# A hybrid decoder step on one core: the samples' state recurrence moved into the input projection, the group norm placed right behind the scan, and branch B taken last in each output tile

## The reference

```
s_kk = S @ kk
S = S * w[None, :] - s_kk[:, None] * (kk * a)[None, :] + v[:, None] * k[None, :]
o = S @ r
```

## Time and profile before

| | |
|---|---|
| median of 3 runs | 1962.02 us (1960.63 to 1970.27) |
| profiled execution | 1961.91 us, span 1960.1 us |
| TensorE busy | 1801.5 us (92%) |
| weight loads | 1092.4 us (56%) |
| VectorE busy | 817.9 us (42%) |
| ScalarE busy | 478.5 us (24%) |
| mean granted TensorE clock | 0.967 |
| DMA | 298.62 MB, mean 152 GB/s |

### The profile page before, as it was taken

How to read it: one execution, slowest core, us unless ns; L and a number is a source line. 1 busy time by engine, 2 the same in 40 slices (tenths; PEclk the granted TensorE clock), 3 DMA queues, 4 the chain that set the end, 5 groups by cost and what they waited for, 6 DMA issues and landing times.

```text
span 1960.1 us, 34623 instructions
## 1 busy us (share of the span) xinstructions
PE 1801.5 (92%) x14642; PEld 1092.4 (56%) x14642; DVE 817.9 (42%) x1662; ACT 478.5 (24%) x855; POOL 170.1 (9%) x220
## 2 busy tenths in 40 slices
PE   6999999999999999979999997887788786999997
PEld 3555555555554556746776775666667342444442
DVE  4450799732213350036556533444434864111112
ACT  4301100010526231125554531111112231100000
POOL 1000000011000005600000000000000001111110
PEclk9999999999999999989999998998989798999999
DMA  6222321385230535141100057777776536878782
GB/s 224 78 105 80 118 87 64 121 196 158 92 120 33 204 153 206 50 152 39 54 1 1 2 175 224 221 236 218 213 226 193 226 100 230 296 272 277 277 297 74
DMA packets 149269, 298.62 MB, mean 152 GB/s; under 512 B 23301, under 2 KB 119349, under 8 KB 130742
## 3 DMA queue, kind: packets, MB, share of 16 engines
q1 hardware_dynamic: 126602, 152.65, 24.7%
q0 software_dynamic: 18240, 115.82, 17.3%
q10 hardware_dynamic: 4272, 27.93, 3.6%
HBM read 234.66 MB, written 63.92 MB: 152 GB/s over the span
## 4 chain that ended last, share of the span: by engine, by line
PE 58%; DVE 17%; SPq 15%; issue 4%; DMA 3%; ACT 3%; POOL 0%; ACTq 0%; DVEq 0%
PE psum L756 23%; PE psum L1257 12%; SPq L525 12%; DVE big L1647 8%; PE psum L908 6%; PE psum L948 4%; PE psum L841 3%; PE psum L919 3%; PE psum L895 2%; SPq L521 2%; PE psum L788 1%; ACT big L1326 1%; PE psum L1242 1%; DMA rkv<-big 1%; DVE big L2029 1%
## 5 line engine op out<-in xcount | busy, mean ns | idle before, releaser
L756 PE MATMUL psum<-big,wbuf 128*128 128x416 f32 x1920 | 675.4, 513 | 3.9 <-DVE big L1577 3.4
L756 PEld LDWEIGHTS psum<-big,wbuf 128*128 128x128 f32 x1920 | 365.0, 190 | 310.7 <-issue 309.0
L948 PE MATMUL psum<-big 64*64 64x64 f32 (+2 forms) x6496 | 269.6, 281 | 48.8 <-DMA big<-in_k_pages 34.0
L948 PEld LDWEIGHTS psum<-big 64*64 64x64 f32 (+1 forms) x6496 | 190.0, 132 | 140.1 <-issue 69.5
L1295 ACT ACTIVATE zst<-psum 128x416 f32<-128x416 f32 x125 | 64.0, 516 | 540.7 <-PE psum L756 540.6
L1257 PE MATMUL psum<-big 128*128 128x512 f32 (+1 forms) x408 | 181.8, 595 | 0.0
L720 POOL DMA_INDIRECT big<-in_cache_v,pidx x64 | 60.7, 949 | 1027.2 <-PE psum L948 1020.5
L1647 DVE SCALAR_TENSOR_TENSOR big<-big,pars 128x2048 f32<-128x2048 f32 x120 | 148.2, 1298 | 1.1
L1257 PEld LDWEIGHTS psum<-big 128*128 128x128 f32 (+1 forms) x408 | 76.2, 187 | 101.4 <-issue 101.4
L2116 DVE TENSOR_TENSOR zst<-zst,psum 128x1024 f32<-128x1024 f32 (+1 forms) x17 | 20.7, 1221 | 224.5 <-PE psum L1257 224.5
L1555 ACT ACTIVATE big<-zst 128x1024 f32<-128x1024 f32 (+1 forms) x17 | 18.0, 1057 | 299.8 <-DVE zst L2116 299.8
(11 more groups left out here) (238 smaller groups left out, 1818.2 us busy)
## 6 DMA issues: line engine op xcount, KB each, us to landing
big<-in_k_pages SPq DMA_DIRECT2D x352, 128.0 KB, 2.3
zT<-zst ACTq DMA_DIRECT2D x25, 1040.0 KB, 6.5
zst<-in_k_pages SPq DMA_DIRECT2D x160, 128.0 KB, 2.4
wbuf<-in_w_slots SPq DMA_DIRECT2D x24, 512.0 KB, 4.5
big<-zT POOLq DMA_DIRECT2D x11, 1024.0 KB, 5.6
rwS<-big POOLq DMA_DIRECT2D x8, 1024.0 KB, 4.2
big<-rwS SPq DMA_DIRECT2D x8, 1024.0 KB, 5.9
zst<-in_x_prompt SPq DMA_DIRECT2D x16, 512.0 KB, 9.2
```

What stands on the lines that cost most here:

```text
L756: last = nc.tensor.matmul(psum[:, m % CHUNKS, 0:CW], w[:, k, :], hT[:, k, c * CW:(c + 1) * CW], start=(k == 0), stop=(k == KT - 1))
L948: return nc.tensor.matmul(out, l, r, start=start, stop=stop, skip_group_check=True)
```

## The change

**The recurrence.** The state is now kept turned: key on the partitions, (sample, tile, value) along 1024 free elements; the host turns the input and output. Decay, key and `kk*a` are then plain columns, broadcast along the free axis (`column`). The value has to be the same on all 64 partitions of a head: the samples' v is turned on TensorE (`turn_samples`, after slot 21), copied by ScalarE, written to DRAM (`zsD`) by four DMAs and read back by SP as four broadcast rows `v_row`. `S @ kk` and `S @ r` become small matmuls: with the key's column, broadcast to 64, as the stationary operand and 64 state columns moving; and with the state stationary and r as a single moving column. Step 0 stands before chunk 4 of slot 23, the others before the value rows 0, 2, 4 and 6. The value rows move from PSUM banks 5 to 7 to banks 0 to 4.

**Queues.** `kq` lies in SBUF where the new state buffers are, so its four loads now stand in SP's queue behind the recurrence's end (`s_done`) and the store of the states. The identity's and the states' loads leave the scan's queue.

**The group norm** begins right behind the scan. Its pieces go by chunk and then tile. The blocks 0 and 1 are turned after the first ten matmuls, blocks 2 to 7 after all thirty; the ten value tiles stand behind them. ScalarE's order is exponentials, squares, copies of blocks 0 and 1, logarithms, exponentials, copies of the rest.

**The output projection** takes A, C, D and then B (`2, 3` last), and waits for B's chunks as a tile needs them.

```diff
+            def turn_samples():
+                pe.wait_ge(made, IDENT)
+                pe.wait_ge(rk_in, 64)
+                pe.wait_ge(lora_read, 20)
+                for t in range(2):
+                    last = transpose(psum[0:SMP, 5, t * P:t * P + P], smp[:, 5, t, :])
+                last.then_inc(lora_mm, 1)
+            def sample_step(i):
+                if i == 0:
+                    pe.wait_ge(lora_read, 21)
+                    pe.wait_ge(s_in, 16)
+                    pe.wait_ge(s_dec, 1)
+                    pe.wait_ge(L_ready, 4)
+                else:
+                    pe.wait_ge(s_ready, i)
+                now = s_wkv[i % 2].rearrange("p (b t v) -> p b t v", b=DEC_BATCH, t=2)
+                if i < DEC_SEQ:
+                    for b in range(DEC_BATCH):
+                        for t in range(2):
+                            for h in range(2):
+                                hs, x = slice(h * 64, h * 64 + 64), b * DEC_SEQ + i
+                                last = nc.tensor.matmul(psum[hs, 5 + b // 4, (b % 4 * 2 + t) * 64:(b % 4 * 2 + t + 1) * 64],
+                                                        smp[hs, 3, t, x:x + 1].to_broadcast([64, 64]), now[hs, b, t, :], start=True, stop=True, skip_group_check=True)
+                    last.then_inc(sk_mm, 1)
+                if i > 0:
+                    for b in range(DEC_BATCH):
...
+                                last = nc.tensor.matmul(psum[hs, 7, t * SMP + x:t * SMP + x + 1], now[hs, b, t, :], smp[hs, 0, t, x:x + 1],
+                                                        start=True, stop=True, skip_group_check=True)
+                    last.then_inc(so_mm, 1)
...
+                    if n == 23 and c == 4:
+                        sample_step(0)
...
+                        if m in (0, 2, 4, 6):
+                            sample_step(1 + m // 2)
                         value_rows(m)
```

VectorE, between its last work on B's inputs and attention's forget sums:

```diff
+            for i in range(DEC_SEQ):
+                dve.wait_ge(x_in[i], X_SEEN[i] + 16)
+                ch.mark(v.tensor_tensor(shape(v_row[i]), shape(v_row[i]), column(2, i), ALU.mult))
+            dve.wait_ge(s_in, 16)
+            dve.wait_ge(s_dec, 1)
+            for i in range(DEC_SEQ):
+                old, new = s_wkv[i % 2], s_wkv[1 - i % 2]
+                if i >= 2:
+                    dve.wait_ge(so_mm, i - 1)
+                ch.link(v.tensor_tensor(shape(new), shape(old), column(1, i), ALU.mult))
+                ch.link(v.tensor_tensor(new, new, v_row[i], ALU.add))
+                dve.wait_ge(sk_mm, i + 1)
+                ch.link(v.tensor_tensor(shape(s_tmp), shape(psum[:, 5:7, :].rearrange("p a b -> p (a b)")), column(4, i), ALU.mult))
+                v.tensor_tensor(new, new, s_tmp, ALU.subtract).then_inc(s_ready, 1)
```

SP's queue, and the tail:

```diff
+            sp.wait_ge(v_spread, 16 * DEC_SEQ)
+            sp.dma_start(s_wkv[0], I['state_T']).then_inc(s_in, 16)
+            for i in range(DEC_SEQ):
+                sp.dma_start(v_row[i], zsD[i].unsqueeze(1).to_broadcast([2, 64, 1024])).then_inc(x_in[i], 16)
...
+            sp.wait_ge(s_done, 1)
+            sp.dma_start(O['wkvT_sample'], s_wkv[0]).then_inc(wkv_stored, 16)
+            sp.wait_ge(wkv_stored, 16)
             for t in range(2):
                 for m, first in ((0, KA), (1, QA)):
                     sp.dma_start(kq[:, m, t, :], zT[first + t]).then_inc(kq_in, 16)
...
             for k, src in enumerate((o_rw, gn_sq, g_rkk)):
-                for t in range(2):
-                    for c in range(CHUNKS):
+                if k == 2:
+                    pe.wait_ge(gn_in, 32)
+                for c in range(CHUNKS):
+                    for t in range(2):
...
-                        if g % 3 == 0:
-                            value_tile(g // 3 - 1)
+                if k == 0:
+                    turn_probs(0)
+                    turn_probs(1)
+            for blk in range(2, 8):
+                turn_probs(blk)
...
+            for n in range(10):
+                value_tile(n)
...
-                for k, e in enumerate((2, 3, 0, 1, 4, 5, 6, 7)):
+                for k, e in enumerate((0, 1, 4, 5, 6, 7, 2, 3)):
+                    if k == 6 and o == 0:
+                        pe.wait_ge(mixb_ready, 2 * ((T * P + n - 1) // CW + 1))
```

More of the change, by code:

```diff
@@ L576, in _ @@
             mix_load(0)
[L577 to L580, removed]
             sp.wait_ge(gn_mm, 4 * CHUNKS)
@@ L750, in chunk @@
                         pe.wait_ge(w_in[n % 2], 16 * max(1, (n + n % 2) // 2))
-                if m >= CHUNKS:
+                if n == N_SLOTS - 1:
+                    pe.wait_ge(vf_evac, max(x for x in range(TT + 1) if x % CHUNKS == c) + 1)
+                elif m >= CHUNKS:
                     pe.wait_ge(z_evac, m - CHUNKS + 1)
@@ L1185, in turn_probs @@
                 last.then_inc(D['pT_tr'], 1)
[L1187 to L1203, removed]
             def value_tile(n):
@@ L1521, in _, with probs_turned @@
             nc.scalar.activation(s_new[:, :], s_new[:, :], ACT.Exp, bias=neg_m[:, :], accum_out=l9[:, 8:9]).then_inc(D['p'], 1)
-            for blk in range(8):
+            def probs_turned(blk):
                 act.wait_ge(D['pT_tr'], D0['pT_tr'] + blk + 1)
@@ L1755, in _, with shape, column @@
             v.memset(vtok[:, TT, 256:VF], 0.0).then_inc(f_pad, 1)
+            def shape(x):
+                return x.rearrange("p (b t v) -> p b t v", b=DEC_BATCH, t=2)
+            def column(m, i):
+                return smp[:, m].rearrange("p t (b i) -> p b t i", i=DEC_SEQ)[:, :, :, i].unsqueeze(3).to_broadcast([P, DEC_BATCH, 2, 64])
+            for i in range(DEC_SEQ):
[3 more added lines that the diff above has]
+            dve.wait_ge(s_dec, 1)
+            for i in range(DEC_SEQ):
+                old, new = s_wkv[i % 2], s_wkv[1 - i % 2]
[6 more added lines that the diff above has]
+                v.tensor_tensor(new, new, s_tmp, ALU.subtract).then_inc(s_ready, 1)
+                dve.wait_ge(s_ready, i + 1)
+            dve.wait_ge(so_mm, DEC_SEQ)
+            v.tensor_copy(o_smp[:, :, :], psum[:, 7, 0:2 * SMP].rearrange("p (t x) -> p t x", t=2)).then_inc(s_done, 1)
             dve.wait_ge(vf_evac, TT + 1)
@@ L2056, in _ @@
-            dve.wait_ge(R['o'], TT)
-            dve.sem_inc(s_done, 1)
+            pieces = [(t, slice(c * CW, (c + 1) * CW)) for c in range(CHUNKS) for t in range(2)]
+            for g, (t, cs) in enumerate(pieces):
+                dve.wait_ge(gn_mm, g + 1)
+                v.scalar_tensor_tensor(o_rw[:, t, cs], psum[:, g % 4, 0:CW], -1.0 / 64, o_rw[:, t, cs], ALU.mult, ALU.add).then_inc(gn_read, 1)
+            dve.wait_ge(a_in, 96)
+            for g, (t, cs) in enumerate(pieces, 4 * CHUNKS):
+                dve.wait_ge(gn_mm, g + 1)
+                v.tensor_tensor(g_v[:, t, cs], psum[:, g % 4, 0:CW], g_v[:, t, cs], ALU.mult).then_inc(gn_read, 1)
@@ L2209 @@
     out = {n: r.results[0]["out_" + n] for n, _ in OUTS}
+    state = np.ascontiguousarray(out['wkvT_sample'].reshape(2, 64, DEC_BATCH, 2, 64).transpose(2, 3, 0, 4, 1))
+    out['wkv_sample'] = state.reshape(DEC_BATCH, 1, 4, 64, 64)
     keys = np.ascontiguousarray(out['kT'].reshape(256, T_ALL).T)
```

192 lines of the change are left out of this document (78 added, 114 removed).

## The result

The changed kernel takes 1973.80 us (median of 20 runs, 1965.78 to 1978.88), the kernel before 1965.38 us beside it (20 runs, 1958.32 to 1974.95): ratio 1.0041, 95% interval 1.0028 to 1.0055. It is slower by 0.4%, within the 0.5% that I had called no change; 1931 us was forecast. The profiled execution is the slowest of the 20 (1978.88 us); it has a span of 1977.1 us (before: 1960.1).

What follows compares the result with a forecast made beforehand. TensorE was taken to bound the kernel (58% of the chain), with VectorE bounding the samples' recurrence and the group norm's tail. Sum: 1961.9 + 17 - 1.5 - 47 = 1930.4, say 1931 us; range 1917 to 1953.

Steps and rivals of the forecast that it cites:

- Step 1: Recurrence under the value-row projection, TensorE: 512 small-product instructions at 29 ns, plus visits and transposes, add 17 us.
- The rivals on the price of small products: Recurrence on TensorE: one-column products at 137 ns add 28 us (1959, 10%); all 512 at 137 ns add 55 (1986, 5%).
- Step 2: VectorE's work and input loads during the value-row projection: inputs there by 753 us, TensorE should not wait; 0, up to 5.
- 5 us of cover: Slack before TensorE asks for step 0's new state at about 766 us; each microsecond later than that costs one.
- The last rival: Recurrence stays on the path: a late state or row load makes TensorE wait in each step; 20 us more, 1951, 3%.
- Step 3: SP's queue in the scan: state and identity loads leave it, saving 1.5 us, between 0 and 2.
- Step 4: Scan's end to output projection: projection starts at 1600 instead of 1646.8 us, gaining 47 us, bounds 35 and 56.
- The projection: Output projection at the kernel's end: same instructions, reordered within each tile with B last; B ready long before, change 0.

Runs made afterwards that it cites:

- halves with tiles: Rows by halves, plus blocks exponentiated and turned last first, each of seven value tiles one turn behind its block; 1914.98 us, 0.9728 of the kernel before in group 4.
- group 4: Runs on one chip beside the kernel before (1965.06 us): rows by halves, halves with tiles, and paced gathers on the latter and on the kernel before.
- By halves: Changed kernel with each broadcast value row loaded by two DMAs of 64 partitions instead of one 2 by 64 load; 1932.90 us in group 4, 2011.81 in group 1.
- paced gathers: Kernel before with each of GpSimd's 64 forget-row gathers issued only when the previous one has landed; 1967.28 us, 1.0011 of the kernel before.
- plain loads: Kernel before with GpSimd's 64 forget-row gathers replaced by plain loads of the same size from fixed places; 1963.48 us, 1.0008 of the kernel before.
- group 2: Runs on one chip: kernel before 2028.26 us, changed kernel 2012.56, rows by halves with late gathers 2005.83, the same with tiles among the turns 1986.60.
- group 1: Runs on one chip: kernel before 2026.83 us, rows by halves 2011.81, halves with tiles 1992.78, and two single runs with other row loads, 2009.01 and 2006.10.

## Why the prediction was wrong

- *Step 1, TensorE's side (+17)*: right. 64 instructions of one column take 1.98 us, 64 of 64 columns 2.08, start to start 1.91 and 1.92 us, 30 ns each (29 predicted). The one column is not dear; the first scores of halves with tiles in group 4 stand at 873.21, 18.2 us behind before's 854.98, and 1.7 of these are the value rows behind the last step (40.8 instead of 39.1 us, granted clock 0.96 instead of 1.00). The rivals on the price of small products fall. The rule of the Trainium skill that the prediction quotes (TensorEngine Tiling (Array Packing), Performance Considerations), that one column costs what 64 do, agrees.
- *Step 2, the queues' side (0, up to 5)*: **the step that failed.** "2.6 MB instead of 4.2 should be there by 753" took the rate from the four 1 MB loads in 12.6 us, which have 128 partitions as their outer dimension. The new loads have an outer dimension of 2 on the source's side and moved 0.5 MB in 12 to 13 us. The last row was used at 804.2 us. By halves it was used at 763.9, in the run of group 4 whose execution was as late by 713 us as this one: 40.3 us earlier. The price was one for one, as I had said, but of the 5 us of cover only 1 to 1.5 were there: 38.4 us of wait, and 5.5 us of half clock behind it that my step did not have. 1931 + 38.4 + 5.5 = 1974.9; measured 1973.8. I had divided bytes by a rate without looking at the shape over which a load is spread. That this load is the whole of the miss is shown by the halves: with it mended and nothing else, 1932.90 us where 1931 was forecast.
- The last rival, "a state or row load lands late", named the mechanism, and mis-sized it: 20 us spread over each step, at 3%. It is one wait of 38 us, because the products with v come for all four rows before step 0; VectorE's order made the last load the one that counts. Taking each row's product into its own step wasn't tried.
- *Step 3 (-1.5)*: first scores to the scan's end 671.5 before, 670.4 after, 1.1 less. It is not shown: the same stretch took 669.6 and 674.3 us in the kernel before with paced gathers and with plain loads, so a term of 1.5 us can't be told in one execution.
- *Step 4 (-47)*: right, 46.7, and its mechanism too (turns, then waits for gathers), but that it is right to 0.3 us is luck: two terms are off and against each other. The turns of blocks 2 to 7 begin 32.0 us behind the mark instead of 35.6 and the last block is turned 48 us behind it (1639.6; 52 predicted), although blocks 4 to 7 run at half clock, 1.94 us each and 3.2 start to start instead of 2.39; first tile to projection is 23.5 us against 20.
- The projection: 312.1 us of span left behind its start, 313.3 before.

## To carry to other kernels

Price a new load by the shape of its access pattern first, then by its bytes: a broadcast written with a small outer dimension took five times as long here as the same bytes by halves, and held the queue behind it for 29 us (eight loads by halves: 5.2 us). Look at which of several loads the first consumer in program order really needs; a loop that prepares all of them first turns the last one's landing into the wait. And when the kernel before runs 3% slower in another group of runs, profile it there before reading any ratio: this change read 1.004 beside a kernel before of 1965 us and 0.992 beside one of 2028.

## What was not expected of the hardware

In two of the groups TensorE's instructions came singly or a few at a time, in the end mostly one per 2.8 us, from 11 to 23 us after GpSimd's 64 indexed gathers began (one per 1.25 us, 80 us in all) until 5 to 9 us after their end, without a semaphore to wait for, and VectorE and ScalarE stood still for 40 us and more; in the others the same stretch ran at full speed (TensorE 50.00 of 50 us from 780 to 830 in halves with tiles of group 4, with 40 gathers in it, against 10.69 in the kernel before of group 2). It cost 62 us in the kernel before (first scores), 67 with the rows by halves (944.76 against 877.77), 70 when the gathers were moved into the attention. That the loss goes where the gathers go is shown by moving them; the same gathers cost nothing in the other groups, so something else has to be there too, and it is not the chip's number (4 in groups 1 and 4). That it is the supply of instructions that they hold up is only argued from the "issue" label; the profile's instruction queues moved one packet between 770 and 836 us by halves in group 1 and five in group 4, which shows them not busy but does not say why.
